# Second half of an output projection by tiles, and a first layer norm by pairs of tiles, in a transformer block

## What is computed

```python
mod = silu(c) @ w_mod + b_mod                       # 6 vectors of 1024
sh1, sc1, g1, sh2, sc2, g2 = split(mod, 6)
u = layer_norm(x) * (1 + sc1) + sh1
merged = ...                                        # attention and convolution branches, gated
out = merged @ w_out
x = layer_norm(ALPHA * x + (1 + g1) * out, ln1_g, ln1_b)      # first norm
u2 = layer_norm(x) * (1 + sc2) + sh2                          # a second norm, without gain
x = layer_norm(ALPHA * x + (1 + g2) * peer(u2, ...), ln2_g, ln2_b)
```

## Time and profile before

| | |
|---|---|
| median of 3 runs | 1676.63 us (1675.67 to 1677.22) |
| the profiled execution | 1672.68 us, its span 1670.9 us |
| mean granted TensorE clock | 0.985 |
| busy: PE, DVE, ACT, POOL | 94%, 81%, 41%, 40% |

### The profile page before, as it was taken

One profiled execution on the slowest core, in us unless ns is written; L12 is line 12 of the kernel. 1 busy time (PEld: TensorE's weight loads), 2 busy tenths in 40 slices (PEclk: granted clock), 3 DMA queues, 4 the chain that ended last, 5 costly groups with the idle time before them and its releaser, 6 DMA issues.

```text
span 1670.9 us, 22384 instructions
## 1 busy us (share of the span) xinstructions
PE 1575.6 (94%) x7902; PEld 1359.4 (81%) x7902; DVE 1357.4 (81%) x2713; ACT 688.9 (41%) x1037; POOL 668.0 (40%) x450
## 2 busy tenths in 40 slices
PE   5999999994999999999999899999999999999896
PEld 3887777773899999999999889889886777777675
DVE  5479786888489899979976889898778788787789
ACT  4344565523334344555553433434323333333342
POOL 0201000002044787687774557475444344453201
PEclk9999999997999999999999999999999999999999
DMA  9223223562567557776779999898889999999962
GB/s 354 101 77 127 89 98 137 169 202 101 203 237 255 139 154 185 204 215 177 189 181 374 350 379 358 333 392 333 328 294 333 395 400 403 402 397 373 373 216 82
DMA packets 180895, 422.24 MB, mean 253 GB/s; under 512 B 33584, under 2 KB 66480, under 8 KB 180528
## 3 DMA queue, kind: packets, MB, share of 16 engines
q1 hardware_dynamic: 90688, 264.44, 43.9%
q0 software_dynamic: 57200, 139.58, 24.4%
q10 hardware_dynamic: 32896, 16.78, 3.6%
HBM read 375.55 MB, written 45.15 MB: 252 GB/s over the span
## 4 chain that ended last, share of the span: by engine, by line
PE 48%; DVE 27%; DMA 9%; POOL 6%; issue 5%; ACT 4%; SPq 0%; DVEq 0%; ACTq 0%
PE bank L1807 14%; PE bank L1808 14%; PE bank L1809 14%; DMA vraw<-in_v_tab_dram 7%; POOL ring L708 6%; DVE wlo L1432 3%; DVE vlo L1652 3%; DVE wf L1640 2%; DVE one L1612 2%; DVE one L1610 2%; ACT eh L997 2%; DMA ring<-in_u_tab_dram,idxN 2%; DVE one L1614 2%; DVE el L1646 2%; DVE ring L1437 2%
## 5 line engine op out<-in xcount | busy, mean ns | idle before, releaser
L1807 PE MATMUL bank<-act_hi,whi 128*128 128x384 f32 (+1 forms) x1352 | 481.4, 356 | 8.4 <-DVE wlo L1432 4.6
L1808 PE MATMUL bank<-act_lo,whi 128*128 128x384 f32 (+1 forms) x1352 | 472.1, 349 | 0.0
L1809 PE MATMUL bank<-act_hi,wlo 128*128 128x384 f32 (+1 forms) x1352 | 472.0, 349 | 0.0
L1807 PE MATMUL bank<-vhi,eh 128*128 128x512 f32 x768 | 305.2, 397 | 22.7 <-DVE vlo L1652 22.6
L1808 PE MATMUL bank<-vlo,eh 128*128 128x512 f32 x768 | 301.4, 392 | 0.0
L1809 PE MATMUL bank<-vhi,el 128*128 128x512 f32 x768 | 301.1, 392 | 0.0
L1807 PEld LDWEIGHTS bank<-act_hi,whi 128*128 128x128 f32 x1352 | 255.2, 189 | 26.8 <-DVE wlo L1432 5.0
L1808 PEld LDWEIGHTS bank<-act_lo,whi 128*128 128x128 f32 x1352 | 255.4, 189 | 13.5
L1809 PEld LDWEIGHTS bank<-act_hi,wlo 128*128 128x128 f32 x1352 | 254.8, 188 | 13.3
L724 POOL DMA_INDIRECT gates_by_key<-selW,selS x128 | 235.0, 1836 | 69.7 <-issue 45.1
L708 POOL DMA_INDIRECT ring<-in_u_tab_dram,idxN x128 | 185.0, 1445 | 131.7 <-DVE ring L1437 78.5
(11 more groups left out here) (249 smaller groups left out, 2027.9 us busy)
## 6 DMA issues: line engine op xcount, KB each, us to landing
raw<-in_u_t_dram SPq DMA_DIRECT2D x128, 512.0 KB, 7.2
vraw<-in_v_tab_dram SPq DMA_DIRECT2D x256, 256.0 KB, 7.7
raw<-in_wblk_dram SPq DMA_DIRECT2D x61, 512.0 KB, 4.2
gring<-gates_by_key SPq DMA_DIRECT2D x32, 768.0 KB, 9.9
raw<-in_w_modt_dram SPq DMA_DIRECT2D x32, 512.0 KB, 3.3
gates_by_key<-stage ACTq DMA_DIRECT2D x8, 2048.0 KB, 13.1
gelu_ahead<-gelz SPq DMA_DIRECT2D x20, 768.0 KB, 4.2
gback<-gelu_ahead SPq DMA_DIRECT2D x40, 384.0 KB, 9.1
```

What stands on the lines that cost most here:

```text
L1807: mm(o, wh, mh, start=start, stop=False)
L1808: mm(o, wh, ml, start=False, stop=False)
L1809: return mm(o, wl, mh, start=False, stop=stop)
```

## The change

- The four weight blocks of half 1 of the output projection get slots of their own (`wo_hi`, `wo_lo`), and `rows_by_tile` takes tile after tile, each with all eight kd. `hi` waits accordingly.
- The first norm: `plus_x` also sums its rows (an accumulator output). `gated(t)` makes the mean from the two sums. ScalarE's `squares` sums (x - mean)^2 over a row of 1024. `variance` and `inverse` follow for the pair of tiles (0, 1) and then (2, 3); `gained` and `first_norm` (VectorE, all four tiles) replace `centred`, `finished` and GpSimd's `gain_bias`. `first_norm` sums its output for the second norm, whose squares ScalarE makes too. `bn` is no longer used here.
- GpSimd has no tensor work left here; its two memsets (`keys`, `zeros`) wait for the end of the projection.
- The modulation dots 16 to 47 stand behind blocks 4 to 7, behind every block from G0 to Y0 and from Y0 to O0 + 3, and none behind later ones: 4, 16, 8 and 4 of them, where it was 8 in G0 to Y0, 8 in Y0 to O0, 8 behind O0 to W0 and 8 behind W0 to the end.
- The parts of W0 + 1 are made ahead of the norm.

The diff, without new semaphores, changed counts of `xa_r`, `root` and `scales` further down:

```diff
@@ -43,13 +43,13 @@
+MOD_AFTER = list(range(4, V0)) + list(range(G0, Y0)) + list(range(Y0, O0)) + list(range(O0, O0 + 4))
 STREAM = []
 for _n in range(NBLK):
     STREAM.append(("w", _n))
-    if G0 <= _n < Y0 and (_n - G0) % 2 == 0:
-        STREAM.append(("mod", (_n - G0) // 2 + 16))
-    elif _n >= Y0:
-        STREAM.append(("mod", _n - Y0 + 24))
+    if _n in MOD_AFTER:
+        STREAM.append(("mod", MOD_AFTER.index(_n) + 16))
+assert len(MOD_AFTER) == MODT - 16
...
@@ -193,6 +193,8 @@
+        wo_hi = sb("wo_hi", [P, 4, D], F32R, 88)
+        wo_lo = sb("wo_lo", [P, 4, D], F32R, 104)
...
@@ -452,6 +457,8 @@
         def w_parts(n):
+            if O0 + 4 <= n < W0:
+                return wo_hi[:, n - O0 - 4, :], wo_lo[:, n - O0 - 4, :]
             return (whi0, wlo0) if n == 0 else (whi[:, n % SPL, :], wlo[:, n % SPL, :])
...
@@ -679,21 +686,10 @@
-            pool.wait_ge(blk_mm, O0)
+            pool.wait_ge(blk_mm, W0)
             nc.gpsimd.memset(keys[:], 0.0).then_inc(const_r, 1)
-            pool.wait_ge(conv_mm, 2)
             nc.gpsimd.memset(zeros[:], 0.0).then_inc(zero_r, 1)
-            def gain_bias(dst, src, rows_of, t):
-                ch.link(nc.gpsimd.tensor_tensor(src[:, t, :], src[:, t, :], rows_of[:, 1, :], ALU.mult))
-                return nc.gpsimd.tensor_tensor(dst[:, t, :], src[:, t, :], rows_of[:, 2, :], ALU.add)
-            pool.wait_ge(row_in, 32)
-            for i, t in enumerate((3, 2)):
-                pool.wait_ge(xa_r, 3 + i)
-                gain_bias(xres, outg, rows1, t).then_inc(x1_p, 1)
-            pool.wait_ge(x1_p, 2)
-            pool.wait_ge(x1_r, 2)
+            pool.wait_ge(x1_r, TT)
             pool.dma_start(x1_dram.rearrange("t p d -> p t d"), xres[:]).then_inc(x1_out, 16)
...
@@ -779,7 +775,12 @@
             def hi(n):
                 s = AT_STREAM[("w", n)]
                 act.wait_ge(raw_in[s % RAW], 16 * (s // RAW + 1))
-                need(act, blk_mm, n - SPL + 1 if n > SPL else 0)
+                if O0 + 4 <= n < W0:
+                    act.wait_ge(blk_mm, O0)
+                elif W0 <= n < W0 + SPL:
+                    act.wait_ge(blk_mm, O0 + 4)
+                else:
+                    need(act, blk_mm, n - SPL + 1 if n > SPL else 0)
                 nc.scalar.activation(w_parts(n)[0][:, :], raw[:, s % RAW, :], ACT.Copy).then_inc(blk_hi, 1)
...
@@ -914,14 +915,31 @@
-            root(2)
-            act.wait_ge(scale_r, 2)
-            for t in (3, 2):
-                scaled(outg, xres, t).then_inc(xa_r, 1)
-            for half in range(2):
-                root(3 + half, slice(2 * half, 2 * half + 2))
-                act.wait_ge(scale_r, 3 + half)
-                scaled(xn, xres, 2 * half + 1).then_inc(xa_r, 1)
+            def squares(t, mean, at, ready, count, done):
+                act.wait_ge(ready, count)
+                nc.scalar.activation(uraw[:, 2 * t:2 * t + 2, :].rearrange("p k c -> p (k c)"), xres[:, t, :], ACT.Square,
+                                     bias=mv[:, t, mean:mean + 1], accum_out=stats[:, t, 0, at:at + 1]).then_inc(done, 1)
+            def normal(t, scaled_by):
+                act.wait_ge(scale_r, scaled_by)
+                scaled(xn, xres, t).then_inc(xa_r, 1)
+            squares(0, 0, 1, ym_r, 1, ysq_r)
+            squares(1, 0, 1, ym_r, 2, ysq_r)
+            root(2, slice(0, 2))
+            squares(0, 1, 3, xm_r, 1, xsq_r)
+            squares(1, 1, 3, xm_r, 2, xsq_r)
+            squares(2, 0, 1, ym_r, 3, ysq_r)
+            root(3, slice(0, 2))
+            squares(3, 0, 1, ym_r, 4, ysq_r)
+            root(4, slice(2, 4))
+            normal(1, 2)
+            squares(2, 1, 3, xm_r, 3, xsq_r)
+            squares(3, 1, 3, xm_r, 4, xsq_r)
+            root(5, slice(2, 4))
+            normal(3, 3)
             modulated(24, 32, KD, KD)
...
@@ -1373,51 +1391,84 @@
             def plus_x(t, half):
                 cut = slice(half * HALF, (half + 1) * HALF)
                 return nc.vector.scalar_tensor_tensor(out=xres[:, t, cut], in0=xres[:, t, cut], scalar=ALPHA,
-                                                      in1=outg[:, t, cut], op0=ALU.mult, op1=ALU.add)
-            def gated(half):
-                if half == 0:
-                    for t in range(TT):
-                        last = gate_bank(t, 0)
-                    link(last)
-                    until(O0 + 7)
-                    for t in range(TT):
-                        last = plus_x(t, 0)
-                    link(last)
-                    for t in range(TT):
-                        bn(xres, t, 0)
-                else:
-                    for t in range(TT):
-                        link(gate_bank(t, 1))
-                        link(plus_x(t, 1))
-                        last = bn(xres, t, 1)
-                    return last
-            for n in range(O0 + 3, O0 + 7):
+                                                      in1=outg[:, t, cut], op0=ALU.mult, op1=ALU.add,
+                                                      accum_out=stats[:, t, half, 0:1])
+            def gated(t):
+                link(gate_bank(t, 1))
+                link(plus_x(t, 1))
+                nc.vector.tensor_scalar(mv[:, t, 0:1], stats[:, t, 0, 0:1], stats[:, t, 1, 0:1], -1.0 / D,
+                                        ALU.add, ALU.mult).then_inc(ym_r, 1)
+            def gained(t):
+                dve.wait_ge(ym_r, t + 1)
+                return nc.vector.scalar_tensor_tensor(out=outg[:, t, :], in0=xres[:, t, :], scalar=mv[:, t, 0:1],
+                                                      in1=rows1[:, 1, :], op0=ALU.add, op1=ALU.mult)
+            def first_norm(t):
+                nc.vector.scalar_tensor_tensor(out=xres[:, t, :], in0=outg[:, t, :], scalar=sq[:, 2, t:t + 1],
+                                               in1=rows1[:, 2, :], op0=ALU.mult, op1=ALU.add,
+                                               accum_out=stats[:, t, 0, 2:3]).then_inc(x1_r, 1)
+                dve.wait_ge(x1_r, t + 1)
+                nc.vector.tensor_scalar(mv[:, t, 1:2], stats[:, t, 0, 2:3], -1.0 / D, None, ALU.mult).then_inc(xm_r, 1)
+            def variance(ts, at, done):
+                dve.wait_ge(done, ts.stop)
+                nc.vector.tensor_scalar(sq[:, 0, ts], stats[:, ts, 0, at], 1.0 / D, EPS, ALU.mult, ALU.add).then_inc(var_r, 1)
+            def inverse(ts, roots):
+                dve.wait_ge(dev_r, roots)
+                link(nc.vector.reciprocal(sq[:, 2, ts], sq[:, 1, ts]))
+                link(nc.vector.tensor_tensor(sq[:, 3, ts], sq[:, 2, ts], sq[:, 2, ts], ALU.mult))
+                link(nc.vector.tensor_tensor(sq[:, 3, ts], sq[:, 3, ts], sq[:, 0, ts], ALU.mult))
+                link(nc.vector.tensor_scalar(sq[:, 3, ts], sq[:, 3, ts], -0.5, 1.5, ALU.mult, ALU.add))
+                link(nc.vector.tensor_tensor(sq[:, 2, ts], sq[:, 2, ts], sq[:, 3, ts], ALU.mult))
+            def second_norm(ts):
+                nc.vector.tensor_tensor(sq[:, 3, ts], mv[:, ts, 1], sq[:, 2, ts], ALU.mult).then_inc(scale_r, 1)
+                t = ts.start
+                nc.vector.tensor_scalar(xn[:, t, :], xres[:, t, :], mv[:, t, 1:2], sq[:, 2, t:t + 1],
+                                        ALU.add, ALU.mult).then_inc(xn_r, 1)
+            for n in range(O0 + 3, W0):
                 until(n)
-            gated(0)
+            for t in range(TT):
+                last = gate_bank(t, 0)
+            link(last)
+            for t in range(TT):
+                last = plus_x(t, 0)
+            link(last)
             until(W0)
+            until(W0 + 1)
             bias(24, 8, False)
             bias(32, 8, True)
             nc.vector.nop().then_inc(mod_r, 1)
-            scales(gated(1), 2, meanwhile=lambda: centred(outg, xres, rows1, 0))
-            finished(xres, outg, rows1, 0).then_inc(x1_r, 1)
-            link(centred(outg, xres, rows1, 1))
-            finished(xres, outg, rows1, 1).then_inc(x1_r, 1)
-            for t in range(2):
-                dve.wait_ge(x1_r, t + 1)
-                bn(xres, t, 0)
-                last = bn(xres, t, 1)
-            scales(last, 3, ts=slice(0, 2))
-            scaled(xn, xres, 0).then_inc(xn_r, 1)
-            for i, t in enumerate((3, 2)):
-                dve.wait_ge(x1_p, i + 1)
-                bn(xres, t, 0)
-                last = bn(xres, t, 1)
-            scales(last, 4, ts=slice(2, 4))
-            scaled(xn, xres, 2).then_inc(xn_r, 1)
-            until(W0 + 1)
+            front, back = slice(0, 2), slice(2, 4)
+            gated(0)
+            gained(0)
+            gated(1)
+            link(gained(1))
+            variance(front, 1, ysq_r)
+            inverse(front, 2)
+            first_norm(0)
+            first_norm(1)
+            gated(2)
+            variance(front, 3, xsq_r)
+            gated(3)
+            inverse(front, 3)
+            second_norm(front)
+            variance(back, 1, ysq_r)
+            gained(2)
+            link(gained(3))
```

(41 more changed lines are left out.)

17 lines of the change are left out of this document (10 added, 7 removed).

## The result

| | before | after |
|---|---|---|
| median (4 runs each) | 1676.88 us (1675.67 to 1677.22) | 1666.01 us (1665.66 to 1668.18) |
| the profiled execution, its span | 1672.68, 1670.9 us | 1668.18, 1666.4 us |
| mean granted TensorE clock | 0.985 | 0.985 |

The ratio of after to before is 0.9935, with a 95% interval of 0.9923 to 0.9946: 10.9 us between the medians, where 9.7 were forecast. The forecast of 1666.9 us is 0.9 us too high.

What follows compares the result with a forecast made beforehand. Bound: a VectorE-ScalarE-GpSimd chain behind the projection's last output tile, which TensorE awaits. Path gain 10.4 us less 0.7 for the clock, dots 0: net 9.7 off the 1676.63 us median gives 1666.9 us; range 1663.5 to 1671.0.

Steps and rivals of the forecast that it cites:

- The bound: End of output projection and first norm: TensorE waits 21.8 us for `xn`, on a chain behind the last output tile.
- Before tile 3: VectorE's work on earlier tiles ends at 383.3, 0.8 us before tile 3, so early work is just hidden.
- The rival that needed VectorE late or tables loaded between squares and roots: First norm: VectorE late before tile 3, small steps dearer, or two table loads on the path, 2.6 us; 1669.5 us, chance 0.12.
- The path after tile 3: From gated(3) to the last transposes, step by step: these begin at 398.8 instead of 409.18, 10.4 us earlier.
- The other signs: First transposes 5 us behind tile 3's gate product, no GpSimd instruction between, low clock at both groups, attention of equal length.
- The clock: Low at both transpose groups; only the second is on the path, sixteen transposes taking 3.42 us, 0.7 us lost.
- the clock stays low: Rival: transposes do not bring the clock back, matmuls from 402 at half speed, 1.5 to 3.4 us lost; chance 0.1.
- The moved dots: Twelve dots of 1.23 us moved into first tiles and attention: taken as 0, bounds nothing and 14.8 us.
- The attention pays: Rival: maxima and exponentials wait for the dots in each head, 14.8 us paid, 1681.7 us; chance of slower 0.03.
- Only a part arrives: Rival: behind this stretch, an earlier start meets other DMA transfers; half the gain, 1671.8 us; chance 0.07.

Runs made afterwards that it cites:

- the dots or the tiles back: Changed kernel with modulation dots in old places, 1672.42 us; or with the projection's second half block by block, 1670.46 us; both against 1676.66 before.
- more work in the attention: Changed kernel plus 14 useless VectorE products of 128x1024 in the first seven attention heads: 1667.27 us against 1677.23 before.
- GpSimd beside the path: Changed kernel plus four idle GpSimd products of 128x1024 right behind tile 3: 1673.86 us against 1676.55 before.

## Why the prediction was right

**The bound.** The wait before the transposes was the place, and the chain behind tile 3 what set it: its end moved by 11.2 us, and 9.6 of it are there at `qT` and at 872 us; the medians differ by 10.9, with some 2 us to each side by the interval, which 9.6 fits.

**Before tile 3.** `gated(0)` was forecast for 369.9 and came at 369.34; tile 1 was ready at 372.97 (373.1), VectorE took the root behind the table load at 377.47 (377.6), and its idle time ahead of tile 3 was 0.85 us (0.8). The rival that needed VectorE late or tables loaded between squares and roots falls with these rows, and the runs with the dots or the tiles back show what lateness would have cost. No wait for `wlo` stands between 362 and 367: the fourth low part was there at 361.35 (358.91 and 2.44), forecast 362.0.

**The path after tile 3.** The forecast was 14.7 us from the product with the gate to the last transposes, and it took 14.13. It lies a little below the 14.5 to 15 us that were to show the forecast right. The 0.6 is spread over the steps, with no more than some 0.2 in any: the two first norms took 2.9 us (390.79 to the square's start at 393.69) instead of 3.0, the squares of tile 3 with their hand-over 1.28 (to 394.97) instead of 1.5, and so on. Tile 3 itself came 0.2 us earlier. So the last transposes gained 11.2 us, not 10.4. The other signs held: the first transposes 5.0 us behind `gated(3)`, low clock at both groups, of GpSimd only the two memsets (0.85 us together, beside `gated(3)`), and ScalarE's conversion behind the first half at 362.14.

**The clock** was the term that was sized wrong. Low at both groups was right, and sixteen transposes at low clock were put at 3.42 us, 0.7 lost. But the 3.42 of the earlier trace rows is not all at low clock: by the earlier trace rows it rose at 407.1, ahead of their end at 407.48. At low clock throughout they took 3.65. And the forecast let them bring the clock back, as in before, while here it was back only at 403.6, so that the first matmuls from 401.28 on took 0.63 us each instead of 0.40 (0.43 from start to start instead of 0.23): 1.57 us lost. That is 0.9 us more than forecast, a little over half of the smaller price (1.5) of the rival "the clock stays low". So in kind it was this rival that came true in this trace, at a smaller price than its own. The two errors, +0.8 and -0.9, cancel to 0.1: 9.7 forecast, 9.6 found. That the sum hits within 0.1 us is luck; either error alone is under 1 us.

The 1.57 is from one execution, the longest of the four. The run with more work in the attention has the same program here, and in its trace it is 14.38 us from the last transposes to `qT`, 0.5 less. What the clock cost in the other executions is not known.

By the rule of the Trainium skill that I set against the trace (TensorE: Matmul & The Clock Gate, Part 4: PE-mode transpose), transposes don't engage the full clock. The rows of after agree with it, where those of before did not: in after neither group brought the clock up, and it rose at 403.6, 2.3 us into the matmuls. Whether sixteen transposes do it differs from trace to trace (below).

**The moved dots** were taken at nothing, between 0 and 14.8 us. Alone they measured 0.15 us faster, with an interval of 2.0 us faster to 0.8 slower. The reason given holds too: in the earlier trace rows a later head had idle time of a dot's length, and in after VectorE's waits for `whi` in the attention fell from 9.5 us (8 waits) to 1.3 (3 waits). The dot lies in that idle time.

**The rivals.** "The attention pays" falls with the runs of the dots alone and of more work in the attention. "Only a part arrives" falls with the medians, whose interval (9.1 to 12.9 us) leaves out half the gain, and with the run with GpSimd beside the path, where about all of 7.9 us arrived; the pair of profiled executions alone would have spoken for it, wrongly.

What the prediction didn't say is how little each part is worth alone: nothing (dots), nothing (dots and tiles), 4.6 us (norm), and 10.9 together. It had the reason for it in its row for VectorE before tile 3: 0.8 us of room there are all there is, and with the dots, the tiles or both undone `gated(3)` begins 4.7 to 6.3 us later, counted from the projection's last matmul.

Two small slips of the prediction change nothing in the sum. Not all DMA transfers of the chain lie behind this stretch: one of 12.35 us stands at 3.6 us, at the kernel's start. And the lower end of the range, 1663.5, lies 3.4 us under the forecast, where 2 us for the small steps were given as its reason.

## What to carry to other kernels

When a chain hangs on the last of several tiles, let the tiles come one by one, and count what the engine behind them must have done before the last one arrives: a norm that can start early, tiles that come early and an engine free early are worth less singly (here nothing to 4.6 us) than together (10.9). Don't add the losses of parts undone one at a time, and don't read a difference of a few us from one profiled execution each. A helper engine may hold up a chain of short instructions by as much as it takes off it; take it out once, and look.
